# Matrix doubling in a recurrence: one head of four computes its q and X in the straight quadrants of TensorE, interleaved with the other heads

## What is computed

```python
def step(state, inp):
    r_t, w_t, k_t, v_t, kh_t, a_t = inp
    removed = jnp.einsum('zhvk,zhk->zhv', state, kh_t)
    state = (state * w_t[:, :, None, :] - removed[..., None] * (kh_t * a_t)[:, :, None, :]
             + v_t[..., None] * k_t[:, :, None, :])
    return state, jnp.einsum('zhvk,zhk->zhv', state, r_t)
```

## Time and profile before

| | |
|---|---|
| median of 3 runs | 3238.83 us (3232.69 to 3241.28) |
| the profiled execution, its own time | 3235.58 us |
| its span | 3233.5 us |
| TensorE busy in the span | 2983.4 us (92%) |
| VectorE busy | 1935.1 us (60%) |
| ScalarE busy | 1248.7 us (39%) |
| the recurrence stage | about 2134 to 2480 us |

### The profile page before, as it was taken

How to read it: one execution, slowest core, us unless ns; L and a number is a source line. 1 busy time by engine, 2 the same in 40 slices (tenths; PEclk the granted TensorE clock), 3 DMA queues, 4 the chain that set the end, 5 groups by cost and what they waited for, 6 DMA issues and landing times. The chain is left out here.

```text
span 3233.5 us, 54557 instructions
## 1 busy us (share of the span) xinstructions
PE 2983.4 (92%) x22430; PEld 2381.1 (74%) x22430; DVE 1935.1 (60%) x2694; ACT 1248.7 (39%) x1579; POOL 895.5 (28%) x469
## 2 busy tenths in 40 slices
PE   9889999999999989999989999759999789999993
PEld 8467888798777767888768777447776468888882
DVE  3756562201444445654299937676564779999996
ACT  3643322222333343232132221512222167777773
POOL 2023444333322213434322210001010033544430
PEclk9989999999999999999989999879999889999996
DMA  4732422322111112222221100320102279999995
GB/s 162 250 108 112 101 94 91 137 91 91 66 66 55 64 65 88 96 92 103 93 77 66 52 32 1 131 96 29 56 29 116 78 275 356 373 365 361 374 365 225
DMA packets 83331, 443.27 MB, mean 137 GB/s; under 512 B 19520, under 2 KB 22592, under 8 KB 34496
## 3 DMA queue, kind: packets, MB, share of 16 engines
q1 hardware_dynamic: 73856, 431.99, 36.6%
q0 software_dynamic: 9280, 8.43, 0.8%
HBM read 425.66 MB, written 39.86 MB: 144 GB/s over the span
## 5 line engine op out<-in xcount | busy, mean ns | idle before, releaser
L78 POOL TENSOR_TENSOR ring_lo<-ring,unit_hi 128x2048 fp32r<-128x2048 f32 x114 | 525.2, 4608 | 1067.7 <-ACT unit_hi L73 1067.7
L139 PE MATMUL wide<-h_hi,unit_hi 128*128 128x512 f32 x1296 | 515.4, 398 | 11.3 <-DVE h_lo L559 4.6
L140 PE MATMUL wide<-h_lo,unit_hi 128*128 128x512 f32 x1296 | 507.0, 391 | 0.0
L141 PE MATMUL wide<-h_hi,ring_lo 128*128 128x512 f32 x1296 | 506.6, 391 | 0.0
L3271 DVE TENSOR_TENSOR ex_w_lo<-ring,ex_w_hi 128x2048 fp32r<-128x2048 f32 x192 | 437.3, 2286 | 44.6 <-ACT ex_w_hi L3221 43.2
L3221 ACT CAST ex_w_hi<-ring 128x2048 fp32r<-128x2048 f32 x192 | 365.5, 1908 | 109.8 <-DMA ring<-in_weights 94.3
L73 ACT CAST unit_hi<-ring 128x2048 fp32r<-128x2048 f32 x116 | 221.4, 1909 | 391.1 <-PE wide L141 386.2
L139 PEld LDWEIGHTS wide<-h_hi,unit_hi 128*128 128x128 f32 x1296 | 244.7, 189 | 71.3 <-issue 12.4
L141 PEld LDWEIGHTS wide<-h_hi,ring_lo 128*128 128x128 f32 x1296 | 244.4, 189 | 51.8
L140 PEld LDWEIGHTS wide<-h_lo,unit_hi 128*128 128x128 f32 x1296 | 244.7, 189 | 48.5 <-issue 0.2
L384 DVE TENSOR_TENSOR ffn_hidden_lo<-ffn_whole,ffn_hidden_hi 128x512 f32 (+1 forms) x44 | 201.2, 4573 | 51.0 <-ACT ffn_hidden_hi L359 51.0
(11 more groups left out here) (521 smaller groups left out, 5895.0 us busy)
## 6 DMA issues: line engine op xcount, KB each, us to landing
ring<-in_weights SPq DMA_DIRECT2D x356, 1024.0 KB, 5.4
rw_F<-factors SPq DMA_DIRECT2D x12, 1024.0 KB, 4.9
factors<-rp_out SPq DMA_DIRECT2D x6, 1536.0 KB, 5.6
tail_both<-pair_rows_out SPq DMA_DIRECT2D x4, 1024.0 KB, 8.4
x<-in_x SPq DMA_DIRECT2D x8, 256.0 KB, 7.3
x_kept<-x SPq DMA_DIRECT2D x1, 2048.0 KB, 12.1
x<-x_kept SPq DMA_DIRECT2D x1, 2048.0 KB, 7.8
x_mixing<-x SPq DMA_DIRECT2D x1, 2048.0 KB, 6.9
```

Of the source, the lines that this page charges most:

```text
L78: pool.tensor_tensor(self.lo[n % RING][:, :], self.ring[n % RING][:, :], self.hi[n % 2][:, :].bitcast(F32), ALU.subtract).then_inc(self.lo ...
L139: pe.matmul(dst, a[0], b[0], start=start, stop=False)
L140: pe.matmul(dst, a[0], b[1], start=False, stop=False)
L141: return pe.matmul(dst, a[1], b[0], start=False, stop=stop)
```

## The change

In each group the last head (`h % 4 == 3`) keeps the halves of X and G in place (`home`, `col`). Its q and its X therefore use the straight quadrants, and their results go to columns 4 and 5 of bank XTB[d] (`straight_x`, `straight_q`). The order of the matmuls of q of slot s and xx of slot s-1 is now interleaved in `q_and_xx`, except where one of the two is in the last level. A new wait, `straight_waits`, stands before q of the straight head, or before all of q in `q_step`: it wants `x_ready[d]` to count every earlier step of the direction. ScalarE copies q in two pieces, VectorE writes X in two, and fills XT with four copies where there were two. The pair mask is one block of 128 columns wider (one DMA, in an earlier stage), and a small buffer, `st`, now lies in `U[0]`.

```diff
+        def crossed(h):
+            return h % 4 != 3
...
+        def home(h, b):
+            return half[1 - b] if crossed(h) else half[b]
...
+        def straight_x(d):
+            return XTB[d][:, 4 * DH:5 * DH]
+        def straight_q(d):
+            return XTB[d][:, 5 * DH:6 * DH]
...
-                def q_step(p, k, d, g):
+                def q_waits(p, k, d, g):
...
-                    for e in range(4):
-                        h = 4 * g + e
-                        dst = QB[:, e * DH:(e + 1) * DH]
-                        if k < LAST:
-                            for b in both:
-                                mm = pe.matmul(dst[half[b]], G[d][half[1 - b], p % 2, h, half[b]], X[d][half[1 - b], p % 2, h, :], start=True, stop=True)
-                        else:
-                            a = source(d)
-                            mm = pe.matmul(dst[half[1 - a]], G[d][half[1 - a], p % 2, h, half[1 - a]], X[d][half[1 - a], p % 2, h, :], start=True, stop=True)
-                    mm.then_inc(q_done[d], 1)
-                def xx_step(p, k, d, g):
+                def q(p, k, d, g, e):
+                    h = 4 * g + e
+                    dst = QB[:, e * DH:(e + 1) * DH] if crossed(h) else straight_q(d)
+                    if k < LAST:
+                        for b in both:
+                            mm = pe.matmul(dst[half[b]], G[d][home(h, b), p % 2, h, first_block(h, b)], X[d][home(h, b), p % 2, h, :], start=True, stop=True)
+                    else:
+                        a = source(d)
+                        mm = pe.matmul(dst[half[1 - a]], G[d][home(h, a), p % 2, h, first_block(h, 1 - a)], X[d][home(h, a), p % 2, h, :], start=True, stop=True)
+                    return mm
+                def straight_waits(p, k, d, g):
+                    if step_no(p, k, g) >= 1:
+                        pe.wait_ge(x_ready[d], step_no(p, k, g))
+                def xx_waits(p, k, d, g):
...
+                def xt(p, k, d, g, e):
+                    h = 4 * g + e
+                    dst = XTB[d][:, e * DH:(e + 1) * DH]
+                    if k < LAST:
+                        for b in both:
+                            mm = pe.matmul(dst[half[b]], Q[d][half[b], h, :], XT[d][half[b], p % 2, h, :], start=True, stop=True)
+                    else:
+                        a = source(d)
+                        mm = pe.matmul(dst[half[a]], Q[d][half[1 - a], h, :], XT[d][half[1 - a], p % 2, h, :], start=True, stop=True)
+                    return mm
+                def x(p, k, d, g, e):
+                    h = 4 * g + e
+                    dst = XB[:, e * DH:(e + 1) * DH] if crossed(h) else straight_x(d)
+                    for b in both:
+                        mm = pe.matmul(dst[home(h, b)], XT[d][half[b], p % 2, h, :], Q[d][half[b], h, :], start=True, stop=True)
+                    return mm
+                def q_step(*step):
+                    q_waits(*step)
+                    straight_waits(*step)
                     for e in range(4):
-                        h = 4 * g + e
-                        x, xt = XB[:, e * DH:(e + 1) * DH], XTB[d][:, e * DH:(e + 1) * DH]
-                        if k < LAST:
-                            for b in both:
-                                pe.matmul(xt[half[b]], Q[d][half[b], h, :], XT[d][half[b], p % 2, h, :], start=True, stop=True)
-                            for b in both:
-                                mm = pe.matmul(x[half[1 - b]], XT[d][half[b], p % 2, h, :], Q[d][half[b], h, :], start=True, stop=True)
-                        else:
-                            a = source(d)
-                            mm = pe.matmul(xt[half[a]], Q[d][half[1 - a], h, :], XT[d][half[1 - a], p % 2, h, :], start=True, stop=True)
-                    mm.then_inc(xx_done[d], 1)
+                        mm = q(*step, e)
+                    mm.then_inc(q_done[step[2]], 1)
+                def xx_step(*step):
+                    xx_waits(*step)
+                    for e in range(4):
+                        mm = xt(*step, e)
+                        if step[1] < LAST:
+                            mm = x(*step, e)
+                    mm.then_inc(xx_done[step[2]], 1)
+                def q_and_xx(step, before):
+                    if step[1] == LAST or before[1] == LAST:
+                        q_step(*step)
+                        xx_step(*before)
+                        return
+                    q_waits(*step)
+                    q(*step, 0)
+                    xx_waits(*before)
+                    xt(*before, 0)
+                    x(*before, 0)
+                    xt(*before, 3)
+                    q(*step, 1)
+                    xt(*before, 1)
+                    x(*before, 1)
+                    straight_waits(*step)
+                    q(*step, 3)
+                    q(*step, 2).then_inc(q_done[step[2]], 1)
+                    xt(*before, 2)
+                    x(*before, 3)
+                    x(*before, 2).then_inc(xx_done[before[2]], 1)
...
-                            q_step(p, k, d, g)
                             if s >= 1:
-                                xx_step(p, k, (s - 1) % 2, (s - 1) // 2)
+                                q_and_xx((p, k, d, g), (p, k, (s - 1) % 2, (s - 1) // 2))
                             elif k >= 2:
-                                xx_step(p, k - 1, 1, 1)
+                                q_and_xx((p, k, d, g), (p, k - 1, 1, 1))
                             elif p >= 1:
-                                xx_step(p - 1, LAST, 1, 1)
+                                q_and_xx((p, k, d, g), (p - 1, LAST, 1, 1))
+                            else:
+                                q_step(p, k, d, g)
...
                         for b in both:
-                            dve.copy_predicated(XT[d][half[b], p % 2, group(g), :],
-                                                masks.level[half[1 - b], 1 - d, 0, :].unsqueeze(1).broadcast_to([DH, 4, DH]),
-                                                G[d][half[1 - b], p % 2, group(g), half[b]]).then_inc(xt_started[d], 1)
+                            dve.copy_predicated(XT[d][half[b], p % 2, 4 * g + 3, :], masks.level[half[b], 1 - d, 0, :],
+                                                G[d][half[b], p % 2, 4 * g + 3, first_block(3, b)])
+                        for b in both:
+                            dve.copy_predicated(XT[d][half[b], p % 2, 4 * g:4 * g + 3, :],
+                                                masks.level[half[1 - b], 1 - d, 0, :].unsqueeze(1).broadcast_to([DH, 3, DH]),
+                                                G[d][half[1 - b], p % 2, 4 * g:4 * g + 3, half[b]]).then_inc(xt_started[d], 1)
                 def grow(p, k, d, g):
                     dve.wait_ge(xx_done[d], step_no(p, k, g) + 1)
                     if k < LAST:
-                        dve.copy_predicated(X[d][:, p % 2, group(g), :], masks.level[:, d, k, :].unsqueeze(1).broadcast_to([P, 4, DH]),
-                                            by_four(XB, 0)).then_inc(x_taken, 1)
+                        dve.copy_predicated(X[d][:, p % 2, 4 * g:4 * g + 3, :], masks.level[:, d, k, :].unsqueeze(1).broadcast_to([P, 3, DH]),
+                                            by_four(XB, 0)[:, 0:3]).then_inc(x_taken, 1)
+                        dve.copy_predicated(X[d][:, p % 2, 4 * g + 3, :], masks.level[:, d, k, :], straight_x(d))
                         dve.copy_predicated(XT[d][:, p % 2, group(g), :], masks.level[:, 1 - d, k, :].unsqueeze(1).broadcast_to([P, 4, DH]),
                                             by_four(XTB[d], 0)).then_inc(x_ready[d], 1)
...
-                    act.copy(Q[d][rows, group(g), :], by_four(QB, 0)[rows]).then_inc(q_ready[d], 1)
+                    act.copy(Q[d][rows, 4 * g:4 * g + 3, :], by_four(QB, 0)[rows, 0:3])
+                    act.copy(Q[d][rows, 4 * g + 3, :], straight_q(d)[rows]).then_inc(q_ready[d], 1)
```

More of the change, by code:

```diff
@@ L2187, in place, with col, first_block @@
             return h % 2 * 4 + h // 2
+        def crossed(h):
+            return h % 4 != 3
+        def home(h, b):
+            return half[1 - b] if crossed(h) else half[b]
+        def col(h, i, wide=1):
+            at = (i if crossed(h) else (i - 1) % 4) * P
+            return slice(at, at + wide * P)
+        def straight_x(d):
+            return XTB[d][:, 4 * DH:5 * DH]
+        def straight_q(d):
+            return XTB[d][:, 5 * DH:6 * DH]
+        def first_block(h, b):
+            at = col(h, 0).start + b * DH
+            return slice(at, at + DH)
         def step_no(p, k, g):
@@ L2287, in pairs @@
                         ar = F[d][rows, p % 2, m, 0:2, :].rearrange("p a t -> p (a t)")
-                        pe.matmul(side[d][h % 2][:, 2 * P:4 * P], F[d][rows, p % 2, m, 3, :], ar, start=True, stop=True).then_inc(pair_done[d], 1)
-                def q_step(p, k, d, g):
```

(11 more changed lines are left out.)

17 lines of the change are left out of this document (9 added, 8 removed).

## The result

| kernel | median of its runs | against the kernel before |
|---|---|---|
| before | 3235.91 us (3232.69 to 3241.28, 5 runs) | |
| after | 3268.61 us (3266.01 to 3277.73, 5 runs) | 1.0103 [1.0088, 1.0117] |

The change costs 33 us. The profiled execution of after is the slowest of the five (3277.73 us, span 3275.6), so its trace shows some 9 us more than the median does; I read from it where the time went, and take how much from the medians. The profiled executions differ by 42.1 us in their spans, and 5.3 us of that lie ahead of the first masks of tile 0 (VectorE starts them at 2127.64 us instead of 2122.33), in work that the change touches only by one wider transfer; it is scatter as far as the other runs tell: in the 16 profiled executions of this document the first q starts anywhere from 2134.1 to 2141.3 us.

The account below looks back on a forecast made before the run. It took TensorE as near the bound, with some slots set by loops between engines and VectorE as full and late in slots 16 to 23. Terms 19 - 5 + 3.7 + 3.5 - 3 = +18.2 gave 3257 us, range 3236 to 3268.

Parts of the forecast that it names:

- five changes of tile: Slots 16 to 2 of the next tile: q waits for late VectorE, net +3.8 us each, +19 in all.
- slots 2 to 15, tiles 1 to 5: Eight slots with enough side work save 0.23 us each, four lose 0.32 each; net -1 per tile, -5.
- tile 0 and the fills ahead of it: Four longer fills before the first slot, +1.7 us, and longer loops through VectorE's normalisation, +2.0; together +3.7.
- end of tile 5: Slots 16 to 23 of the last tile: q, xx and `grow` follow one another, +3.5 us.
- issue gaps now hidden: TensorE's standstill for its own issue, 21.5 us ahead of XT alone, partly falls under the waits: -3 us.
- bare slots: Slots without side work (6, 9, 12, 13): the new wait makes them 1.56 us instead of 1.24, +0.32 each.
- rival 1: Fill of XT: its copies overlap, 0.15 us more instead of 0.42; +11.6, so 3250 us; 15 in 100.
- theory B: Whole stage, from the follow-up experiments: the loss is the clock, which falls behind long waits.
- Rival 2: Slots 16 to 1: VectorE keeps up, stalls go, array saving -26.6 us; about -10, 3229 us; chance 0.13.
- Rival 3: Whole stage: stalls fall where TensorE stood still anyway, or side work quickens; within 0.3%, 3240 us; chance 0.14.
- Rival 4: Slots' matmul pairs stop running together in the mixed order; about +50 us, 3290 us; chance 0.03.

Follow-up runs that it names:

- wait_only: The kernel before with only the new TensorE wait for `grow` of two slots back added ahead of q; 3273.85 us, 1.0105.
- after_pool: The changed kernel, wait and order kept, with GpSimd making the fills of XT of tiles 1 to 5; 3250.24 us, 1.0031.
- before_pool: The kernel before with GpSimd instead of VectorE making the fills of XT of tiles 1 to 5; 3237.26 us, 0.9994.

## Why the prediction was wrong

It said slower, 3257 us within 3236 to 3268; slower was right, and the median is 3268.6. The sum was +18.2 us and the medians differ by 32.7. Term by term, from the profiled executions:

| term | predicted | measured |
|---|---|---|
| five changes of tile | +19 | +26.2 |
| slots 2 to 15, tiles 1 to 5 | -5 | +4.0 |
| tile 0 and the fills ahead of it | +3.7 | +2.9 in its slots, +0.7 ahead |
| end of tile 5 | +3.5 | +3.5 |
| issue gaps now hidden | -3 | none seen |
| products behind the last XT | 0 | +2.5 |
| ahead of the first masks of tile 0, scatter as far as known | 0 | +5.3 |
| behind the products, scatter as far as known | 0 | -3.0 |

**The step that failed** is "Slots 2 to 15 of tiles 1 to 5: eight with enough side work save 0.23 each (-1.9); slots 6, 9, 12, 13 lose 0.32 each, less what `finish` already costs there (+0.9)", which gave -5 where the trace has +4.0. Both halves were wrong. The saving, 9.5 us over five tiles, came to 3.8 in all slots that are not bare: it was counted wherever TensorE ends the slot, without asking which quadrants end it, and where a straight tail of side work stands ahead, moving pairs from crossed to straight quadrants bought nothing (+0.09 us in slot 3, -0.02 in slot 4). The loss in the bare slots, 4.5 us, came to 7.9, and in slot 12 it came by another path: not through the new wait and `grow`, but through q and ScalarE, whose loop I had at 1.38 us and which takes 1.42. `wait_only` adds that the wait costs 7.9 us in slots 2 to 15 by itself, but not in bare slots 6 and 12 (1.27 and mostly 1.24 us); slots 7, 10 and 13 pay most of it. Together this step is 9 us of the miss in the trace; the third change of tile, under the clock, is 4.5 more, and the 3 us of issue that I had hidden under the waits are not gained.

**The changes of tile** were right in mechanism and nearly in size: counted from the start of `grow` for slot 17, q of slot 20 came at 4.3 us (4.6 predicted), of slot 21 at 7.65 (8.1), of slot 0 at 15.7 (15.4), of slot 2 at 20.7 (20.0). Three of the five cost 3.8 to 4.4 us more than the matching one before (3.8 predicted), the fourth 5.0. The third cost 8.8, with a clock of 0.69 in its window. Of the four fills ahead of tile 0 only two are finished before its first q, so that 0.7 us show there and not 1.7. The fill, at 0.34 us more where GpSimd writes nothing beside it (0.47 + 0.77 with 0.05 between and behind, 1.29 for 0.95), was between my bounds and near the upper one; rival 1 is out: the four take 0.47 and 0.77 us one behind another. The pieces of `grow` do overlap (0.38, 0.22 and 0.44 us long, starting at 2336.58, 2336.85 and 2336.98); why those of the fill don't, no run here shows.

**The clock** had no term. What it costs where nothing waits shows in the products behind the last XT, the same 186 matmuls in both kernels, windows of before and of after:

```profile
2463.91:2475.16 11.25, 11.15 (x186) 8.54 (x184) 0.43 (x2) 3.62 (x8) 0.00 (x0) 1.00 0.01 4
```

```profile
2506.57:2520.27 13.70, 13.60 (x186) 10.21 (x184) 0.43 (x1) 3.63 (x8) 0.00 (x0) 0.80 0.01 2
```

0.20 x 13.70 x 2 = 5.5 us at half speed go with 13.70 - 11.25 = 2.45 us more. The stretch before it is the end of tile 5, where TensorE is busy for 10.3 of 14.9 us. In the third change of tile, with the waits of the others, the clock of 0.69 goes with 4.5 us more than the mean excess of the other four. These two are some 7 us of this one execution. The mean over the stage says little: the stage of `after_pool` has 0.92 too, which is 53 us at half speed, 32 of them in tile 0, and it takes 333.9 us, 4.4 more than that of before. So theory B is not the main cause; how much of the 33 us between the medians the clock is stays open, since it differs from one execution to the next and no run here held it still.

**Rivals.** Rival 2 (VectorE keeps up, 3229) is out by the time; what it would have brought could be tried, since in `after_pool` VectorE keeps up. Its changes of tile fell below those of before, and yet it took 3250: the -26.6 us that the rival counted for the array are not there, not even at the changes of tile, where `before_pool` is within 1.1 us of it. Rival 3 is out by 1.0103. Rival 4 (pairs stop running together) is out: q, XT and X pairs of slot 8 stand 0.06 us apart, and the slot got 0.22 us shorter. The two halves of a pair still write one bank together: the 16 passes of slot 0's q, 12 of them into one bank, take 0.56 us (2389.65).

The loss by medians, the terms as the runs price them: wait +34 us, fills +9, q's copy +2 and not told from nothing, together 45; change without interleaving +56. So the parts seem to make each other worse; a likely reason is that a longer fill delays a `grow` that is now waited for, but no run adds the parts one by one. Interleaving -23. What the shorter array is worth alone is in no run: without interleaving slot 8 takes 2.10 us of the 2.16 before, so most of its 0.22 comes with the order.

## What to carry to other kernels

In the kernel before VectorE was late, q hardly waited for it (4.3 us in 13 waits of levels 1 to 5), and a new wait for it cost 33 us (1.0105): read how late it is (its end against the first use of what it makes) before adding the wait, and try the wait alone on the old kernel. A saving on the array was worth 0.22 us in slot 8 and nothing in slot 3, behind a straight tail: ask for each slot which quadrants end it and what stood in them just ahead. Where two engines are nearly equally full, as here with 20.4 and 21.6 us of a change of tile's 22.0, lightening one may give little (0.9994), and loading it cost about in full (9 us). Make the control of a repair, too: without `before_pool` the gain at the changes of tile would have passed for the array's.

## What the runs showed of the hardware

- A fill of XT on VectorE, SBUF to SBUF, took 0.47 us for its two 64-wide pieces in after, but 1.01 us (two fills) and 0.78 us (four) where GpSimd wrote X and XT at the same time. VectorE and GpSimd at the fourth change of tile:

```profile
2387.27 1.01 DVE L2567 COPY_PREDICATED rw_XT<-level_mask,rw_G 64x64 f32<-64x64 uint32 x2
```

```profile
2387.03 0.61 POOL L2251 COPY rw_X<-half_ident 128x512 f32<-128x512 f32 x1 [4.66 <-PE wide L2361]
```

- GpSimd did the same fill with multiplications and additions, 64x256 each in 0.72 us (29.0 us for 40 of either in `before_pool`), and in the traces of `before_pool` and `after_pool` TensorE waits for none of it at the changes of tile.
- The granted clock of the third change of tile was 0.69, and 0.94 to 1.00 in the other four, which have the same work and the same waits: it was at 0.50 from 2297.0 to 2303.8 and from 2314.1 to 2331.2 us. Ahead of both falls TensorE stood still in part: it was busy for 0.71 of the 2.0 us ahead of the first, and for 2.32 of the 4.0 us ahead of the second (from 2310.1). In the first two changes it was busy for 2.30 and 2.32 of 4.0 us at the same place (from 2192.45 and from 2250.79), and the clock stayed at 1.00. Why it fell in the third and not there no run shows.
